# Stick-breaking attention in a one-core layer kernel: the order of masks, copy-outs and slots

## The reference

```
z = jnp.einsum('bhtd,bhsd->bhts', qh[:, :, start:end], kh[:, :, :end])
mask = jnp.arange(end)[None, :] < jnp.arange(start, end)[:, None]
log_1m = jnp.where(mask, jax.nn.log_sigmoid(-z), 0.0)
suffix = lax.cumsum(log_1m, axis=3, reverse=True) - log_1m
a = jnp.where(mask, jnp.exp(jax.nn.log_sigmoid(z) + suffix), 0.0)
outs.append(jnp.einsum('bhts,bhsd->bhtd', a, vh[:, :, :end]))
```

## Time and profile before

| | us |
|---|---|
| median of 3 runs | 3914.02 (3913.75 to 3915.89) |
| the profiled execution | 3910.47 |
| its span | 3908.7 |
| the phase of the change in it, first score product to the last copy-out | 463.5 to 711.3 |

### The profile page before, as it was taken

How to read it: one execution, slowest core, us unless ns; L and a number is a source line. 1 busy time by engine, 2 the same in 40 slices (tenths; PEclk the granted TensorE clock), 3 DMA queues, 4 the chain that set the end, 5 groups by cost and what they waited for, 6 DMA issues and landing times.

```text
span 3908.7 us, 35644 instructions
## 1 busy us (share of the span) xinstructions
PE 3189.3 (82%) x10072; PEld 1663.8 (43%) x10072; DVE 2324.4 (59%) x5493; ACT 1640.7 (42%) x4273; POOL 1596.6 (41%) x1176
## 2 busy tenths in 40 slices
PE   6798788977887888888888888888787777877777
PEld 5577533666666443434333444443222222222222
DVE  3343344234334777776776676676667667667665
ACT  2121377223222555544544444454444444444443
POOL 0000011000000556444555445445765766666765
PEclk8899899988988999999999999999999999999999
DMA  2101000221023999999999999999999999999998
GB/s 77 35 24 43 0 1 1 87 97 43 23 76 121 416 409 419 417 415 414 414 414 414 417 410 415 413 408 412 420 414 408 420 405 420 416 415 420 414 407 353
DMA packets 173010, 1147.66 MB, mean 294 GB/s; under 512 B 19472, under 2 KB 21536, under 8 KB 41632
## 3 DMA queue, kind: packets, MB, share of 16 engines
q0 software_dynamic: 147456, 1073.81, 66.8%
q1 hardware_dynamic: 25376, 71.87, 5.1%
HBM read 1141.41 MB, written 4.19 MB: 293 GB/s over the span
## 4 chain that ended last, share of the span: by engine, by line
DMA 29%; POOL 9%; PE 9%; issue 7%; ACT 7%; DVE 6%; POOLq 0%; ACTq 0%; DVEq 0%
DMA expert_rows<-in_uv,expert_index 29%; POOL expert_rows L1433 9%; PE expert_acc L1905 8%; DVE expert_rows L1660 4%; ACT expert_dg L1778 1%; ACT expert_wt L1775 1%; ACT L1774 1%; ACT expert_wt L1774 1%; ACT L1694 1%; DVE expert_w_lo L136 1%; ACT expert_w_hi L131 1%; DVE expert_hot L1523 0%; ACT expert_best L1694 0%; ACT L1720 0%; ACT expert_spare L1720 0%
## 5 line engine op out<-in xcount | busy, mean ns | idle before, releaser
L1905 PE MATMUL expert_acc<-expert_rows,expert_dg 128*128 128x512 f32 x4096 | 2010.6, 623 | 485.4 <-ACT expert_dg L1778 484.6
L1433 POOL DMA_INDIRECT expert_rows<-in_uv,expert_index x1024 | 1547.1, 1511 | 1094.2 <-PE expert_acc L1905 809.1
L1660 DVE CUSTOM_DVE_ANT_0 expert_rows<-expert_rows,expert_xn 128x1024 f32<-128x1024 f32 x1024 | 1254.8, 1225 | 719.5 <-DMA expert_rows<-in_uv,expert_index 716.3
L1905 PEld LDWEIGHTS expert_acc<-expert_rows,expert_dg 128*128 128x128 f32 x4096 | 737.6, 194 | 1606.4 <-ACT expert_dg L1778 1004.9
L1774 ACT ACTIVATE expert_wt<-expert_dot 128x1 f32<-128x1 f32 x1024 | 207.4, 203 | 1329.9 <-DVE expert_dot L1660 1327.6
L1778 ACT ACTIVATE expert_dg<-ident,expert_wt 128x128 f32<-128x128 f32 x1024 | 411.2, 402 | 33.7
L1775 ACT ACTIVATE expert_wt<-expert_wt,expert_gate 128x1 f32<-128x1 f32 x1024 | 301.3, 294 | 33.4
L1425 POOL IOTA expert_iota<- 128x16 f32 x1 | 0.1, 144 | 534.8 <-PEq L1793 534.8
L905 POOL TENSOR_SCALAR_AFFINE_SELECT heads<-heads 128x128 f32<-128x128 f32 x64 | 20.7, 324 | 331.6 <-DVE heads L958 331.3
L958 DVE SCALAR_TENSOR_TENSOR heads<-stick_pz,stick_t 128x512 f32<-128x512 f32 (+3 forms) x96 | 53.2, 557 | 134.0 <-ACT stick_t L943 133.8
L1774 ACT ACT_TABLE_LOAD x79 | 101.4, 1283 | 7.3 <-DVE expert_dot L1660 6.0
(11 more groups left out here) (367 smaller groups left out, 4182.0 us busy)
## 6 DMA issues: line engine op xcount, KB each, us to landing
expert_rows<-in_uv,expert_index POOLq DMA_INDIRECT x1024, 12.4
H<-in_x SPq DMA_DIRECT2D x8, 1024.0 KB, 10.3
pq_w_raw<-in_w_pq SPq DMA_DIRECT2D x16, 512.0 KB, 3.3
expert_w_raw<-in_w_pq SPq DMA_DIRECT2D x32, 256.0 KB, 8.9
stick_w_raw<-in_w_feat SPq DMA_DIRECT2D x8, 512.0 KB, 3.3
tok_w_raw<-in_w_tok SPq DMA_DIRECT2D x8, 512.0 KB, 4.0
out_w_raw<-in_w_out SPq DMA_DIRECT2D x8, 512.0 KB, 5.3
mk_w_raw<-in_w_mk SPq DMA_DIRECT2D x8, 512.0 KB, 5.0
```

Of the source, the lines that this page charges most:

```text
L1433: pool.indirect_dma_start(out=rows[R % ROWS], out_offset=None, in_=uv, in_offset=bass.IndirectOffsetOnAxis(ap=index[:, q, r:r + 1], axis=0 ...
L1660: nc.vector.tensor_tensor_reduce(rows[R % ROWS][:, 0:D], rows[R % ROWS][:, 0:D], xn[:, :], 1.0, 0.0, ALU.mult, ALU.add, dot[:, h % 2, r:r ...
L1905: last_mm = nc.tensor.matmul(acc[:, h * HALF:(h + 1) * HALF], dg[:, r % DG, :], rows[(TOPK * (PH * b + g) + r) % ROWS][:, D + h * HALF:D + ...
```

## The change

Three orders change; no instruction is added or removed. GpSimd masks the weights of slot i - 2 ahead of the new sums of slot i. VectorE's copy-out stands first in its turn. And the first slot of the next pair changes places with the slot (0,1) of the pair before: slots 10 and 11 become (0,0,1) and (1,1,7), slots 22 and 23 and slots 34 and 35 likewise. Pair 0 begins as before, and the last two slots stay the last.

```diff
-    rounds = [(0, 1, 7), (-1, 0, 1), (0, 1, 6), (-1, 0, 0), (0, 1, 5), (0, 1, 4), (0, 0, 3), (0, 1, 3), (0, 0, 2),
+    rounds = [(-1, 0, 1), (0, 1, 7), (0, 1, 6), (-1, 0, 0), (0, 1, 5), (0, 1, 4), (0, 0, 3), (0, 1, 3), (0, 0, 2),
               (0, 1, 2), (0, 1, 1), (0, 1, 0)]
...
             for i in range(M + 2):
+                for n in (2 * i - 4, 2 * i - 3):
+                    if n >= 0 and diag[n]:
+                        pool.wait_ge(a_ready, n + 1)
+                        strict(aw[:, n % S, :], tile(n)[3], a_masked)
                 for m in (2 * i, 2 * i + 1):
                     if i < M and diag[m]:
                         pool.wait_ge(sp_ready, m + 1)
                         strict(sps[:, m % S, :], tile(m)[3], sp_masked)
-                for n in (2 * i - 4, 2 * i - 3):
-                    if n >= 0 and diag[n]:
-                        pool.wait_ge(a_ready, n + 1)
-                        strict(aw[:, n % S, :], tile(n)[3], a_masked)
...
             for i in range(M + 5):
+                n = 2 * (i - 4) + 1
+                if 0 <= n < N and tile(n)[2] == 0:
+                    pr, th, _, _ = tile(n)
+                    dve.wait_ge(pv_done, n + 1)
+                    hi, lo = (x[:, GLA_HEADS + pr, th * HALF:(th + 1) * HALF] for x in mix_t)
+                    nc.vector.tensor_copy(hi, po[th][:, :]).then_inc(hi_ready, 1)
+                    dve.wait_ge(hi_ready, ended.index((pr, th)) + 1)
+                    low(nc, lo, po[th][:, :], hi).then_inc(o_free, 1)
                 two = (2 * i, 2 * i + 1) if i < M else ()
...
-                n = 2 * (i - 4) + 1
-                if 0 <= n < N and tile(n)[2] == 0:
-                    pr, th, _, _ = tile(n)
-                    dve.wait_ge(pv_done, n + 1)
-                    hi, lo = (x[:, GLA_HEADS + pr, th * HALF:(th + 1) * HALF] for x in mix_t)
-                    nc.vector.tensor_copy(hi, po[th][:, :]).then_inc(hi_ready, 1)
-                    dve.wait_ge(hi_ready, ended.index((pr, th)) + 1)
-                    low(nc, lo, po[th][:, :], hi).then_inc(o_free, 1)
```

## The result

| | before, us | after, us |
|---|---|---|
| median of the runs | 3914.23 (3913.75 to 3915.89, 4 runs) | 3866.95 (3865.40 to 3870.68, 4 runs) |
| the profiled execution | 3910.47 | 3867.17 |
| phase of the change | 463.5 to 711.3: 247.8 | 462.9 to 669.8: 206.9 |
| rest of the profiled execution | 3662.7 | 3660.3 |

The ratio is 0.988, with a 95% interval from 0.9863 to 0.9897. The change saves 47.3 us between the medians, where 39.3 were forecast; 3866.95 lies 1.05 us under the lower end of the range, 3868. Between the two profiled executions it is 43.3 us, 40.9 of them in the phase.

The account below looks back on a forecast made before the run. In the stick-breaking phase the tensor engine (PE) and ScalarE share the bound. Savings 17.8 + 8.0 + 8.0 + 3.0 + 3.4 - 0.9 = 39.3 us; 3914.02 - 39.3 = 3874.7 us, range 3868 to 3886.

Parts of the forecast that it names:

- The clock behind it: Low granted clock after the boundary idles goes, 8.0 us saved; 2.67 us idles left it up at boundaries two and three.
- the median of the runs is 3.55 us above that execution: Offset from the profiled execution, 3910.47 us, to the median of the runs, giving 3914.02 us as the base.
- Copy-out and order: At three pair boundaries PE's 5.93 us wait for the copy-out before the value product goes whole: 17.8 us saved.
- Masks of the weights: Value products' waits for GpSimd's masks go: three of 2.67 us at boundaries, 8.0 us; three of 1.01 us elsewhere, 3.0 us.
- The opening: PE's waits for masks at the phase's start go; ScalarE, the nearer bound, regains 3.4 us (0 to 5.8).
- What is late next: First mask of slot 13's new sums comes late behind the copy-out at each boundary: 0.9 us against (0 to 4.2).
- The carry waits: Slot 12's carry must wait for slot 11's sums; VectorE may lose up to 6.3 us, off the path.
- Masks that meet a carry add: Moved GpSimd masks may take 0.55 us instead of 0.29; nothing counted, 1.6 us less by the shared-port rule.
- case A: The main forecast: all terms hold, 39.3 us saved, 3874.7 us; chance 0.68.
- B: Rival: PE catches up and waits for the second head's masks at boundaries, 6.7 us; saving 32.6, 3881.4 us; chance 0.19.
- C: Rival: mask order gives nothing, since slot 15's sums wait for all masks; 23.4 us saved, 3890.6 us; chance 0.09.
- D: Rival: slower, VectorE waits for PE's value product at eight copy-outs; 8 us slower, 3922 us; chance 0.03.

Follow-up runs that it names:

- copy_twice: Changed kernel with the first half of each copy-out done three times at the head of VectorE's turn: 3872.8 us, phase 214.3 us.
- masks_only: Kernel before with only the mask order changed: 3894.5 us, phase 231.0 us.
- no_masks: Changed kernel with the mask order as before, slot order and copy-out still changed: 3890.1 us, phase 231.7 us.
- copy_only: Kernel before with only the copy-out moved to the head of VectorE's turn: 3892.9 us, phase 229.9 us.
- order_only: Kernel before with only the slot order changed: 3895.1 us, phase 233.8 us.
- no_copy: Changed kernel with the copy-out last in VectorE's turn as before, mask and slot order still changed: 3877.4 us, phase 219.5 us.
- no_order: Changed kernel with the slot order as before, mask order and copy-out still changed: 3873.3 us, phase 212.5 us.
- after_again: The changed kernel run once more, in five rounds beside the kernel before: 3866.83 us against 3915.05, ratio 0.9879.

## Why the prediction was wrong

The mechanism stood in its parts, and so did the direction. The term that failed is **"The clock behind it"**, sized 8.0 us with "bounds 0 and 8.0", and with it the sentence that in the second and third boundary "the 2.67 us idle left the clock up". In the profiled execution the clock did cost 8.7 us of PE's busy time (211.9 - 203.3), but in three others of the same kernel it cost 17.8 to 18.7. The upper bound was taken from one execution, for a cost that differs between executions. With a phase of 256.2 us the gain in it is 49.3, 8.4 more than the 40.9. The 2 us between this and the 47.3 of the medians are within what the remainder varies by: its mean is 3658.4 us in these three, it is 3660.3 and 3659.3 in two profiles of the changed kernel, and lies between 3657.6 and 3664.2 over all kernels profiled without padding.

A second step hid it: "the median of the runs is 3.55 us above that execution" was carried over as a constant. It was the difference of two larger ones, a phase 8 us shorter and a remainder some 4 us longer than usual. An offset between a profile and the median belongs somewhere, and if it lies in what the change removes, it goes with it.

Step by step, in the first profile's own terms:

- *Copy-out and order, 17.8 us:* right, the wait is gone. Leaving either half out brings back waits of 1.96 or 2.79 us; the two are needed together for zero.
- *Masks of the weights, 8.0 and 3.0 us:* right for the kernel before. That without it two further waits for masks would come out at each boundary, once the wait for the copy-out is short, the prediction did not see. This cost nothing, since the parts came together, but it makes the mask order the part that is worth more behind the other two (24.8 us) than alone (16.8).
- *The opening, 3.4 us:* 3.65 measured. ScalarE's turn 5 starts on the scores (L941) at 482.13 - 462.90 = 19.2 us into the phase, before at 486.41 - 463.53 = 22.9.

```profile
481.18 1.06 ACT L934 ACTIVATE tok<-stick_pz 128x512 f32<-128x512 f32 x2
482.13 0.60 ACT L941 ACTIVATE stick_t<-stick_pz 128x512 f32<-128x512 f32 x1
```

- *What is late next, -0.9 us:* the new sums of slot 13 are late, but PE's gap in front of its sums is 0.1 us, not 0.3. The carry waits do not show on PE.
- *Masks that meet a carry add:* they do, 0.44 and 0.72 us for one and two in the turn at 523.23 us of the changed kernel, and no PE wait follows. The rule of the Trainium skill on the shared port pair (SBUF — State Buffer, the section on the two separate sides) cost nothing on the path here: PE waited 0.3 us for masks of the weights in the whole phase, where 1.6 us was the estimate by that rule with both masks caught.
- *Rivals:* what happened is case A. B would have shown waits for masks of new sums; there is one, 0.9 us, in the opening as before. C falls with the wait for the weights' masks at 0.3 us and PE idle of 3.6 us in all. D falls: VectorE waited for PE's value product at one copy-out, the last of the phase, for 4.0 us, and just as long in the kernel before. The margin is another matter: copy_twice shows that the room behind the copy-out at a boundary is 0.5 us.

The sum of the phase was 1.6 us short of the 40.9 measured in the first profile, all small terms. Against the other three profiles the 8.0 us for the clock were 9.8 to 10.7 us too little, and that made the miss.

## What to carry to other kernels

When a stall is priced, the clock behind it is part of the price, and one profile does not bound it: compare the busy time of the same instructions over several executions before taking it. Waits of engines that run in fixed order cover one another, so a part is worth one thing alone and another behind the others (here 17.9 and 12.6 us for the copy-out, 16.8 and 24.8 for the masks); ask of each part which waits the other parts uncover. In a loop where every engine works on several stages in a turn, try putting first what the bounding engine asks for first, as both moves here did, and test the room that is left by doubling the moved work.

## What was not expected of the hardware

- Executions of the kernel before differ in one phase: PE busy 211.9 us in one profile, 221.0 to 222.0 in three, for the same 736 records, with idles at the boundaries equal to 0.01 us. After idles of 5.93 us the clock was low in all four profiles and in masks_only, 15 of 15. After idles of 2.67 us it stayed up twice in the first profile and fell in the other 10 places of the four; in no_masks, copy_only and order_only it fell in 5 of 9. After the idles of 2.79 us in no_copy it fell in two of three places, after the six of 1.96 us in no_order and copy_only in none. But the length of one idle does not settle it: in copy_twice idles of 0.96 and 0.52 us, 0.44 us of work apart, were followed by the low clock at one boundary of three. What decides in between was not found.
- The changed kernel, with no idle over 1 us in the phase once it has started, repeats in the phase to 0.1 us over three profiles (203.3, 203.2, 203.2 us of PE), and its four times in the comparison of after_again lay within 1.1 us, where 17 of the kernel before covered 10. In the first comparison its four times covered 5.3 us, so the narrow spread is not a rule.
